# Attention scores as three products of split operands, with the vector engine's tail of a head in another order

## What is computed

```python
q = apply_rope(q, cos, sin) * (DA_DH ** -0.5)
k = apply_rope(k, cos, sin)
def block(q_blk):                       # 128 queries
    s = jnp.einsum('bhmqd,bhmkd->bhmqk', q_blk, k).astype(jnp.float32)   # m: 2 maps, d: 64
    p = jax.nn.softmax(s, axis=-1)
    a = p[:, :, 0] - lam * p[:, :, 1]
    return jnp.einsum('bhqk,bhkv->bhqv', a.astype(v.dtype), v)
```

## Time and profile before

| | |
|---|---|
| time, median of 3 runs | 2473.77 us (2473.47 to 2474.88) |
| time of the profiled execution | 2470.46 us |
| its span, first to last instruction | 2468.5 us |
| PE busy | 2451.6 us (99%) |
| PE weight load busy | 2262.7 us (92%) |
| DVE busy | 1830.1 us (74%) |
| ACT busy | 1281.3 us (52%) |
| POOL busy | 185.3 us (8%) |
| granted TensorE clock, mean | 0.999 |
| chain that ended last | PE 92%, DVE 3%, ACT 2% |

### The profile page before, as it was taken

The page is one execution under the profiler, slowest core; times in us unless marked ns, Lnnn a source line. Parts: engine busy times, 40 slices in busy tenths (PEclk is TensorE's granted clock), DMA queues, the critical chain, the costliest instruction groups (busy, mean ns, idle before and its releaser), DMA issues.

```text
span 2468.5 us, 41237 instructions
## 1 busy us (share of the span) xinstructions
PE 2451.6 (99%) x16634; PEld 2262.7 (92%) x16634; DVE 1830.1 (74%) x2427; ACT 1281.3 (52%) x1970; POOL 185.3 (8%) x236
## 2 busy tenths in 40 slices
PE   9999999999999999999999999999999999999998
PEld 9999989898899999888899998898889999998887
DVE  6656777754788999978575567776648888999784
ACT  4444666543355555556444456664424555564563
POOL 0001011100200000003100011011002000000031
PEclk9999999999999999999999999999999999999999
DMA  5354434254322233834233544343543232347421
GB/s 171 124 187 133 142 131 144 88 179 161 103 71 88 75 102 110 307 102 138 96 119 127 173 150 138 123 133 115 179 145 101 69 92 82 95 149 261 149 99 60
DMA packets 290267, 321.53 MB, mean 130 GB/s; under 512 B 10400, under 2 KB 223904, under 8 KB 290080
## 3 DMA queue, kind: packets, MB, share of 16 engines
q1 hardware_dynamic: 215744, 171.39, 22.5%
q10 hardware_dynamic: 74336, 147.53, 16.5%
HBM read 253.60 MB, written 65.27 MB: 129 GB/s over the span
## 4 chain that ended last, share of the span: by engine, by line
PE 92%; DVE 3%; ACT 2%; issue 1%; DMA 1%; POOL 1%; SPq 0%; ACTq 0%; POOLq 0%; DVEq 0%
PE ps L853 21%; PE ps L1140 14%; PE ps L1321 13%; PE ps L1076 9%; PE ps L811 6%; PE ps L1059 5%; PE ps L1427 5%; PE ps L1261 3%; PE ps L825 3%; PE ps L1287 2%; PE ps L1029 2%; PE ps L1407 1%; PE ps L911 1%; PE ps L1048 1%; PE ps L1009 1%
## 5 line engine op out<-in xcount | busy, mean ns | idle before, releaser
L853 PE MATMUL ps<-hT_hi,whi 128*128 128x384 f32 x608 | 204.1, 336 | 1.0 <-ACT U L2964 0.6
L853 PE MATMUL ps<-hT_lo,whi 128*128 128x384 f32 x608 | 203.1, 334 | 0.0
L853 PE MATMUL ps<-hT_hi,wlo 128*128 128x384 f32 x608 | 203.1, 334 | 0.0
L2007 DVE TENSOR_TENSOR wlo<-raw,whi 128x1024 fp32r<-128x1024 f32 (+1 forms) x154 | 165.4, 1074 | 41.9 <-ACT whi L2949 41.9
L2964 ACT ACTIVATE U<-ps 128x384 f32<-128x384 f32 x152 | 74.7, 492 | 218.4 <-PE ps L853 218.4
L1321 PE MATMUL ps<-whi,PH_hi 128*128 128x512 f32 x456 | 179.0, 393 | 0.0
L1321 PE MATMUL ps<-whi,PH_lo 128*128 128x512 f32 x456 | 177.7, 390 | 0.0
L1321 PE MATMUL ps<-wlo,PH_hi 128*128 128x512 f32 x456 | 177.5, 389 | 0.0
L1505 DVE TENSOR_TENSOR wlo<-raw,whi 128x2048 fp32r<-128x2048 f32 x53 | 122.3, 2307 | 68.1 <-ACT whi L2328 68.0
L1609 DVE TENSOR_TENSOR wlo<-raw,whi 128x1024 fp32r<-128x1024 f32 (+1 forms) x98 | 102.8, 1069 | 77.2 <-ACT whi L2490 77.1
L853 PE MATMUL ps<-S_hi,whi 128*128 128x384 f32 x456 | 152.5, 334 | 0.0
(11 more groups left out here) (318 smaller groups left out, 7039.7 us busy)
## 6 DMA issues: line engine op xcount, KB each, us to landing
raw<-w_up_dram SPq DMA_DIRECT2D x88, 512.0 KB
raw<-w_in_dram SPq DMA_DIRECT2D x64, 512.0 KB
raw<-w_down_dram SPq DMA_DIRECT2D x60, 512.0 KB, 4.6
raw<-w_in_dram SPq DMA_DIRECT2D x16, 1024.0 KB
zT<-gst ACTq DMA_DIRECT2D x40, 384.0 KB, 2.4
GT<-zT ACTq DMA_DIRECT2D x16, 768.0 KB, 5.8
pD<-CG ACTq DMA_DIRECT2D x26, 384.0 KB, 2.3
zT<-hn ACTq DMA_DIRECT2D x48, 192.0 KB, 1.8
```

The costliest lines, as they stand in the source:

```text
L853: ins = mm(ps[:, 4 * (j % 2) + bank, 0:TH], quarter(L, W[y], j, (w,))[:, 0, k * P:(k + 1) * P], sum_operand(a, x, k), start=(opens and k = ...
L2007: v.tensor_tensor(quarter(L, wlo, j, names), raw_quarter(j, names), quarter(L, whi, j, names).bitcast(F32), ALU.subtract)\
```

## The change

Scores: the rotated `QK` is split like other operands. `QK_hi` (an ACT copy, over the place of `QKs`) and `QK_lo` (a DVE subtraction, over `QK` itself) take the place of `QK` in L1029, and each map of each block becomes three fp32r matmuls in place of one float32 matmul; the two maps alternate. PE waits for the step "low" where it waited for "radd".

Order: on DVE, in the tail of a head, `far_up` goes ahead of the second rotation product; the sum of the rotation goes ahead of `gla_forget` and `gla_keys`; the low part comes behind `gla_keys`; and in `gla_output` the sum of squares goes ahead of the copy "o". At the start of a layer the low part stands ahead of the layer constants. On ACT the high part stands ahead of `merge_keys(it + 1, 0)` in the tail, and behind the last stores and ahead of `load_v` at the start of a layer.

```diff
-    out = ["o", "ss", "on", "ab0", "ab1"]
+    out = ["ss", "o", "on", "ab0", "ab1"]
...
+        QK_lo, QK_hi = stack(x_off, h_off, [("QK_lo", [P, 2, T], F32R), ("QK_hi", [P, 2, T], F32R)])
...
-        A_rope = steps("att_rope", ["cqk", "sqk", "radd"])
+        A_rope = steps("att_rope", ["cqk", "sqk", "radd", "low"])
+        A_high = steps("att_rope_high", ["high"])
...
             def att_scores(it, q):
                 k0, kn = SEQ_OF[q]
                 if q == 0:
-                    pe.wait_ge(A_rope.sem, A_rope.at(it, "radd"))
+                    pe.wait_ge(A_rope.sem, A_rope.at(it, "low"))
...
-                for m in range(2):
-                    rows_ = slice(m * DA_DH, (m + 1) * DA_DH)
-                    ins = mm(ps[:, AB[m], 0:kn], QK[rows_, 0, q * P:(q + 1) * P], QK[rows_, 1, k0:k0 + kn], start=True, stop=True)
+                for i, (x, y) in enumerate(PASSES):
+                    for m in range(2):
+                        rows_ = slice(m * DA_DH, (m + 1) * DA_DH)
+                        ins = mm(ps[:, AB[m], 0:kn], (QK_hi, QK_lo)[y][rows_, 0, q * P:(q + 1) * P], (QK_hi, QK_lo)[x][rows_, 1, k0:k0 + kn],
+                                 start=(i == 0), stop=(i == 2))
...
             def gla_output(it):
                 done(G_sq, it, "sq")
+                v.tensor_reduce(st_g[:, 0, :], SQ1[:], AX_X, ALU.add).then_inc(*G_out.step("ss"))
                 v.tensor_copy(O1[:], view(ps[:], GB[0] * 512, [[P, NT], [1, P]])).then_inc(*G_out.step("o"))
-                v.tensor_reduce(st_g[:, 0, :], SQ1[:], AX_X, ALU.add).then_inc(*G_out.step("ss"))
...
+            def att_rope_low(it):
+                done(A_high, it, "high")
+                v.tensor_tensor(QK_lo[:], QK[:], QK_hi[:].bitcast(F32), ALU.subtract).then_inc(*A_rope.step("low"))
...
                 v.tensor_reduce(st_t[:, 0, :], SQ2, AX_X, ALU.add).then_inc(*A_dve.step("ss"))
+                far_up(it)
                 if following:
                     att_rope(it + 1, L, "sqk")
-                far_up(it)
-                if following:
-                    gla_forget(it + 1)
                 done(A_pool, it, "rs")
                 v.tensor_tensor(O2[:], O2[:], view(st_t[:], 2 * NT, [[1, NT], [0, P]]), ALU.mult).then_inc(*A_dve.step("on"))
                 if following:
+                    att_rope(it + 1, L, "radd")
+                    gla_forget(it + 1)
                     gla_keys(it + 1)
-                    att_rope(it + 1, L, "radd")
+                    att_rope_low(it + 1)
                 gla_output(it)
...
+                att_rope_low(L * NH)
                 dve.wait_ge(s_lay, L * 48 + 48)
...
+            def att_rope_high(it):
+                done(A_rope, it, "radd")
+                a(QK_hi[:], QK[:], ACT.Copy).then_inc(*A_high.step("high"))
...
                 if following:
+                    att_rope_high(it + 1)
                     merge_keys(it + 1, 0)
...
                 in_store_rest(L, I1 - 1)
+                att_rope_high(L * NH)
                 load_v(L, 0)
```

## The result

| | before | after |
|---|---|---|
| median | 2473.47 us | 2487.0 us (2483.3 to 2489.0) |
| span of the profiled execution | 2468.5 us | 2485.2 us |
| granted TensorE clock, mean | 0.999 | 0.995 |

What follows compares the result with a forecast made beforehand. PE was taken to bound the kernel, busy 2451.6 of 2468.5 us. Tails 14.0, starts 8.2, scores -8.2 and 0.4 of their gain hidden sum to +14.4 us: 2488 us against the median, range 2477 to 2507.

Steps and rivals of the forecast that it cites:

- six tails: Ends of heads: PE waits 2.2, 2.6 and 2.2 us for copy "o" before the diagonal, 14.0 us over both layers.
- two starts, chain: Start of each layer's heads: the low part waits for ACT's high part and delays DVE's chain, 4.1 us twice, 8.2.
- scores, net of what the starts hide: Score blocks: paired fp32r products gain 0.21 us at 512 keys, 0.09 at 256, -8.2 in all; 0.4 hidden at starts.
- clock: PE's granted clock, mean 0.999 of 2.4 GHz before: the main forecast's sum included no loss from it.
- The list of 10.9 us: Tail of a head: DVE's steps from the scaling's start through copy "o", without a pause, take 10.9 us.
- rival 3: Behind eight gaps of 2 to 4 us the clock falls to 1.2 GHz: +17 us, 2505 us; 10%.
- Rival 4: Tails and starts: DVE's large operations run faster in the new order, no gaps come; -8.2 us, 2466 us; 7%.

Runs made afterwards that it cites:

- the maps in turn: Kernel after with all three score products of map 0 ahead of those of map 1, instead of alternating: 2484.2 us, ratio 1.0054 to the kernel before.
- all rows: Kernel after with all 128 rows in each score product, so both maps hold the summed scores (computation changed): 2502.2 us, ratio 1.0121 to the kernel before.

## Why the prediction was right, and which terms were not

The time came out 1 us from the forecast, and that closeness is luck: the tails cost 4 us less than forecast, and the clock, put at nothing, cost 7. What was right is the mechanism of the tails, the starts and the scores. The terms, forecast against the shift of PE's points in the two traces:

```
                                       forecast   measured
six tails                                +14.0       +9.7
two starts, chain                         +8.2       +7.7
scores, net of what the starts hide       -7.8       -6.3
clock                                        0       +6.9
waits ahead of head 1's far products         0       -1.1
sum                                      +14.4      +16.9
```

Over the heads of both layers PE's points move by 17.0 us, so the terms account for them. The spans differ by 16.7, because outside the heads the two executions differ too. The 384 products of a dense stage (L811, L813 in the kernel after) take 67.67 us in both layers before and in layer 0 after, but 66.41 in layer 1 after. A new wait of 0.5 us at L1325 and smaller shifts make up for most of it. Both values come in the traces of other kernels of this study as well. What decides between them is open; by this alone the span of one trace can differ from another's by 1.3 us a layer.

- **The list of 10.9 us** was right to 0.02 us, and so were the place of the wait and its releaser.
- **The tails' gaps** were forecast too large by 0.6, 1.0 and 0.8 us (2.2, 2.6 and 2.2 against 1.62, 1.62 and 1.38). The step that failed is that the scaling at L1764 stays where it is. In the earlier trace rows it stands at 301.84; after, at 306.16, 4.32 us later, where PE's points around it had moved by 4.91. So in head 0 DVE's list began 0.6 us sooner against PE, and 2.2 became 1.6. The cause is POOL's pair of small operations, in front of the scaling. Before, with the rotation product on DVE beside the first and `far_up` and `gla_forget` beside the second, they take 1.53 and 1.75 us:

```profile
298.44 1.53 POOL L2242 TENSOR_SCALAR st_t<-st_t 128x6 f32<-128x6 f32 x1 [50.00 <-DVE st_t L1757]
300.05 1.75 POOL L2244 TENSOR_TENSOR st_t<-st_t,half_neg 128x6 f32<-128x6 f32 x1
```

  After, 0.20 and 1.33, and the scaling waits only for DVE's own queue. The run with the product first again brought the slow first operation back (1.53) and half of the miss (waits of 11.6 us in six, against 9.2 after and 14.0 forecast): that half is shown. The other half goes with the second operation, 1.75 us before and 1.38 in that run, and is only read from the traces. I had put the move of `far_up` among those that change nothing, and said of POOL only that it is idle in the rest of the tail. The Trainium skill, page "GPSIMD Engine Reference", section 1, says that VectorE and GpSimd share access to SBUF and get in each other's way during VectorE instructions with two SBUF inputs; the trace agrees, and it is the small POOL operation that pays here, 1.3 us.
- **Head 1** gives back 1.0 us in layer 0 (from +5.78 at the side piece to +4.76 at the transposes) and 0.65 in layer 1; 0.3 of each is lost again at the products behind the transposes. PE before, in that tail:

```profile
367.40 1.99 PE L996 MATMUL ps<-QP,KS 128*128 128x256 f32 x8 [0.36 <-DVE QP L1676]
...
369.62 0.87 PE L1015 MATMUL ps<-ident,O 128*128 128x128 f32 x6 [0.22 <-DVE O L1764]
```

  With `far_up` ahead of the product both waits are gone in the trace after. They were too short to stand in the rows that I had chosen.
- **The starts** were right: 3.8 to 3.9 us each where 4.1 was said. The low part does hold up DVE's chain, as the run with only the starts mended confirms.
- **The scores.** The mechanism was right (in pairs, the fixed part stays); the size of a pass was off. I took 0.21 us for 512 columns, and between the second and the third pair it is 0.23: a block takes 0.89 us, not 0.85, a gain of 0.17, not 0.21. The earlier trace rows had 0.22.
- **The clock** was rival 3. It said eight falls, 17 us; four came, 6.9 us: 1.8 and 2.2 at the starts, 1.4 at each of head 1's tails, the other four gaps without. The run with filled gaps, whose clock stays up, shows that idleness of PE was the cause. What tells a tail with a fall from one without, at the same gap of 1.6 us, is open. It does not hang on the kernel alone: the five executions of the kernel after have mean clocks from 0.995 to 0.997 and took 2489.0 down to 2483.3 us. So where another kernel's trace has its falls elsewhere (none in the tails with the maps in turn or with all rows, heads 1 and 2 with the rotation first), one trace does not show that the edit moved them. The Trainium skill, page "TensorE: Matmul & The Clock Gate", Part 1, says that an idle TensorE falls back to 1.2 GHz; the starts agree as to the level, with 0.50 granted behind 2.41 us of idleness.

Rival 4 was closer than it looked: the faster order it spoke of exists, but on POOL, and was worth 0.4 us a tail in the run that takes it back, 0.6 to 1.0 by the traces, not 2.2.

## What to carry to other kernels

When an engine at 99% gets cheaper work, price first the operations that prepare it on the other engines, at the places where they stand ahead of something that the busy engine awaits; here 6 us of gain came with 17 us of waits, and with the low part a few places later at the starts, the tail in nearly its old order and the copy on ACT, PE waited for none of it. A copy that frees a buffer goes ahead of everything that only later steps need, or to an engine with time to spare. And when large operations change places, look at the small ones on POOL beside them: here one took 0.20 us or 1.53.

## What the hardware showed that I had not expected

- The two halves of the array run their products side by side whatever the order in the program: with the maps in turn, the first product of map 1 starts with the first of map 0 although two of map 0 stand ahead of it (block of 0.90 us, alternating 0.89). The Trainium skill, page "TensorE: Matmul & The Clock Gate", Part 3, says that matmuls start and end strictly in program order; here this does not hold across the halves, and the measurement decides. At which point in front of the array they are taken apart, the trace does not say.
- An operation on six columns on POOL took 0.20 us or 1.53, and a power on six columns 1.33, 1.75 or 2.71, by what DVE did beside it. Where it took 1.53, it ended 0.06 us behind DVE's product both times (299.97 and 299.91 before, 305.50 and 305.44 with the rotation first), as if it had waited for that end.
- Four clock falls that cost 1.4 to 2.2 us each came behind gaps of 1.6 to 2.4 us, some 7 us in a kernel whose mean clock still reads 0.995.
- The same 384 products of a dense stage took 67.67 us in some executions and 66.41 in others, at a granted clock of 1.00 both times.
